# A mixed-layer kernel: most of the products into channel-by-token form, with the weights standing in the array

## The reference

```
block 1: u = rmsnorm(x) * norm_w;  proj = mm(u, w_in)
  split -> ml_q, ml_k, ml_v, ml_o, ml_z, gates, dn_q, dn_k, dn_v, dn_z, gate_a, gate_b
  mLSTM: 8 heads, q.k scores with gate decays, times v, norm, sigmoid(o)*silu(z)
  delta rule: causal conv of 4 taps over tokens on dn_q, dn_k, dn_v, then silu,
     l2norm of q and k, 16 heads in chunks, triangular solve, norm, silu(z)
  x = rmsnorm(x + sigmoid(gate_a)*mm(h_a, w_out[:2048]) + sigmoid(gate_b)*mm(h_b, w_out[2048:]))
block 2: h = rmsnorm(x)*w;  aq, ak, av, gq, gk, gv, gr, gl = split(mm(h, w_in_2))
  dilated window attention, 16 heads of 64 (aq, ak, av); gated linear attention, 4 heads (gq, gk, gv)
  x = x + mm([attention, gla], w_out_2);  h = rmsnorm(x)*w
  x = x + mm(silu(mm(h, w_gate)) * mm(h, w_up), w_down);   out = rmsnorm(x)*w
```

## Time and profile before

| what | value |
|---|---|
| time, median of 3 runs | 2382.64 us (2382.16 to 2382.72) |
| time of the profiled execution | 2382.65 us |
| its span | 2380.8 us |
| granted TensorE clock | 0.999 |
| busy PE / DVE / ACT / POOL | 2364.4 / 1425.4 / 1184.1 / 241.6 us |

### The profile page before, as it was taken

The page is one execution under the profiler, slowest core; times in us unless marked ns, Lnnn a source line. Parts: engine busy times, 40 slices in busy tenths (PEclk is TensorE's granted clock), DMA queues, the critical chain, the costliest instruction groups (busy, mean ns, idle before and its releaser), DMA issues.

```text
span 2380.8 us, 28492 instructions
## 1 busy us (share of the span) xinstructions
PE 2364.4 (99%) x11458; PEld 1938.3 (81%) x11458; DVE 1425.4 (60%) x1701; ACT 1184.1 (50%) x1695; POOL 241.6 (10%) x336
## 2 busy tenths in 40 slices
PE   9999999999999999999999999999999999999998
PEld 7888888888788888888887778788888888888886
DVE  5655665665566545665864565576554554557775
ACT  6544453454445444555645455465444444446654
POOL 0053004305300430000000010000000000000000
PEclk9999999999999999999999999999999999999999
DMA  6565457446535655666665454456555555555554
GB/s 211 194 174 164 142 177 186 155 156 182 171 127 187 177 165 168 221 207 198 209 218 191 142 179 146 155 178 226 188 187 194 189 184 193 194 181 192 193 195 141
DMA packets 240658, 430.81 MB, mean 181 GB/s; under 512 B 32180, under 2 KB 35133, under 8 KB 240526
## 3 DMA queue, kind: packets, MB, share of 16 engines
q1 hardware_dynamic: 227536, 413.38, 54.4%
q10 hardware_dynamic: 12990, 15.60, 2.1%
HBM read 423.66 MB, written 5.29 MB: 180 GB/s over the span
## 4 chain that ended last, share of the span: by engine, by line
PE 89%; POOL 5%; DVE 2%; DMA 1%; issue 1%; ACT 1%; ACTq 0%; SPq 0%; POOLq 0%; DVEq 0%
PE gemm L1311 27%; PE gemm L1313 27%; PE gemm L1312 27%; POOL arena L2264 5%; PE side L893 3%; DMA arena<-delta_blocks 1%; DVE arena L1732 1%; DVE weight_lo L1726 1%; PE side L1234 1%; PE side L981 0%; PE side L903 0%; PE side L1249 0%; PE side L1273 0%; ACT weight_hi L1339 0%; PE side L1047 0%
## 5 line engine op out<-in xcount | busy, mean ns | idle before, releaser
L1726 DVE TENSOR_TENSOR weight_lo<-weight_raw,weight_hi 128x1024 fp32r<-128x1024 f32 x780 | 969.7, 1246 | 733.5 <-ACT weight_hi L1339 732.2
L1339 ACT ACTIVATE weight_hi<-weight_raw 128x1024 fp32r<-128x1024 f32 x780 | 821.9, 1056 | 860.9 <-PE gemm L1313 820.3
L1311 PE MATMUL gemm<-weight_hi,x_hi 128*128 128x512 f32 x2368 | 942.1, 398 | 3.3 <-DVE x_lo L1732 2.1
L1313 PE MATMUL gemm<-weight_hi,x_lo 128*128 128x512 f32 x2368 | 923.1, 390 | 0.0
L1312 PE MATMUL gemm<-weight_lo,x_hi 128*128 128x512 f32 x2368 | 922.1, 389 | 0.0
L1311 PEld LDWEIGHTS gemm<-weight_hi,x_hi 128*128 128x128 f32 x2368 | 444.7, 188 | 103.4 <-issue 12.5
L1313 PEld LDWEIGHTS gemm<-weight_hi,x_lo 128*128 128x128 f32 x2368 | 444.4, 188 | 94.3
L1312 PEld LDWEIGHTS gemm<-weight_lo,x_hi 128*128 128x128 f32 x2368 | 445.1, 188 | 89.4 <-issue 1.4
L1311 PE MATMUL gemm<-weight_hi,lhs_hi 128*128 128x512 f32 x736 | 287.1, 390 | 0.0
L1313 PE MATMUL gemm<-weight_hi,lhs_lo 128*128 128x512 f32 x736 | 286.4, 389 | 0.0
L1312 PE MATMUL gemm<-weight_lo,lhs_hi 128*128 128x512 f32 x736 | 286.3, 389 | 0.0
(11 more groups left out here) (184 smaller groups left out, 1028.4 us busy)
## 6 DMA issues: line engine op xcount, KB each, us to landing
weight_raw<-in_w_in_dram SPq DMA_DIRECT2D x207, 1024.0 KB, 5.1
weight_raw<-in_w_out_dram SPq DMA_DIRECT2D x48, 1024.0 KB, 5.1
weight_raw<-in_w_gate_dram SPq DMA_DIRECT2D x44, 1024.0 KB, 5.2
weight_raw<-in_w_up_dram SPq DMA_DIRECT2D x44, 1024.0 KB, 5.2
weight_raw<-in_w_down_dram SPq DMA_DIRECT2D x44, 1024.0 KB, 5.0
arena<-rel_line ACTq DMA_DIRECT2D x8, 384.0 KB, 6.1
arena<-in_x_dram SPq DMA_DIRECT2D x4, 512.0 KB, 9.5
arena<-delta_blocks ACTq DMA_DIRECT2D x16, 128.0 KB, 5.2
```

What stands on the lines that cost most here:

```text
L1311: e.matmul(pair[i][:, :], xh[:, s], wh, start=first, stop=False)
L1313: m = e.matmul(pair[i][:, :], xl[:, s], wh, start=False, stop=last)
L1339: return e.activation(o, i, ACT.Copy, scale=scale)
L1726: return e.tensor_tensor(o, x, y, op)
```

## The change

Products of the kinds dk, dq, dv, mq, mk, gq, gk, aq, ak, fg and fu (44 jobs, list `ACROSS`) are made with 128 weight columns standing and 256 tokens moving, so that their results come with channels on the partitions. The first product of each of a job's two banks streams 256 tokens and 256 zeros (a new block `x_hi[KD]`), which opens the whole bank. The turns of these jobs (`convturn`, `chan` on PE, `fturn`) go. The norm's scale is now wanted along the free axis in every partition: `rdiag` puts the scales on the diagonal of a 128 by 128 matrix (DVE), `rrow` multiplies it by ones on PE, and DVE copies the result to `scale_rows`. DVE evicts with this row (`conv`, `chan`, `fgate`), in place of `kept` on ACT and DVE and the copies behind the turns. In the feed-forward `tanh` and `silu` read the evicted gate from SBUF, and `fact` multiplies by fu's banks and then by the row.

```diff
-    put(6, "nscale", "x")
+    put(6, "nscale", "x"), put(6, "rdiag", "x"), put(7, "rrow", "x")
     put(6, "cols")
     def kept_conv(key, slot):
-        put(slot, "kept", key)
+        put(slot, "conv", key)
         for c in (0, 2):
-            put(slot + 1, "convturn", key, c)
-            put(slot + 2 + c, "convtap", key, c)
-        put(slot + 5, "convsilu", key)
+            put(slot + 1 + c, "convtap", key, c)
+        put(slot + 4, "convsilu", key)
...
-    put(s, "nscale", "r1"), put(s, "nscale", "x2")
+    put(s, "nscale", "r1"), put(s, "nscale", "x2"), put(s, "rdiag", "x2"), put(s + 1, "rrow", "x2")
...
+            put(s + 5, "rdiag", "r2"), put(s + 6, "rrow", "r2")
     for n in range(FFN // NC):
-        put(END[f"fg{n}"], "tanh", f"fg{n}"), put(END[f"fg{n}"] + 1, "silu", f"fg{n}")
-        s = END[f"fu{n}"]
-        put(s, "fact", n), put(s + 1, "fturn", n, 0), put(s + 1, "fturn", n, 2)
+        put(END[f"fg{n}"], "fgate", n), put(END[f"fg{n}"], "tanh", f"fg{n}"), put(END[f"fg{n}"] + 2, "silu", f"fg{n}")
+        put(END[f"fu{n}"], "fact", n)
...
+        def rrow(tag):                                                       # PE
+            w.wait_ge(*at("dve:rdiag", tag))
+            p, d = open_bank("rrow", tag), blk("diag", tag)
+            for i in range(NT):
+                m = e.matmul(p[:, i * P:(i + 1) * P], ONE, d[:, i * P:(i + 1) * P], start=True, stop=True)
+            m.then_inc(sem("pe:rrow"))
...
+                if kind_of(name) in ACROSS:                                  # PE, product
+                    for q in range(NC // P):
+                        o, s = pair[q // 2][:, q % 2 * T:(q % 2 + 1) * T], slice(q * P, (q + 1) * P)
+                        if first and q % 2 == 0:
+                            e.matmul(pair[q // 2][:, :], wh[:, s], xhi[:, 0:KD + 1:KD, :], start=True, stop=False)
+                        else:
+                            e.matmul(o, wh[:, s], xh, start=False, stop=False)
+                        e.matmul(o, wh[:, s], xl, start=False, stop=False)
+                        m = e.matmul(o, wl[:, s], xh, start=False, stop=last and q % 2 == 1)
+                    continue
...
+        def conv(key):                                                       # DVE
+            x = claim("raw", key)
+            w.wait_ge(*at("dve:rrow", "x"))
+            w.wait_ge(*out_of(key))
+            for i in range(2):
+                s = tt(by_row(part(x, i)), by_row(pair_of(key)[i][:, :]), over(rrows[:, :], 1, 2), ALU.mult)
+            s.then_inc(sem("dve:conv"))
...
+        def chan(key):                                                       # DVE; aq reads the tokens backwards
+            for i in range(2):
+                    s = stt(ch[:, 2 * i:2 * i + 2, :], p, scale, over(rrows[:, :], 1, 2), ALU.mult, ALU.mult)
...
+        def fgate(n):                                                        # DVE
+            for i in range(2):
+                s = tt(by_row(part(z, i)), by_row(pair_of(f"fg{n}")[i][:, :]), over(rrows[:, :], 1, 2), ALU.mult)
...
         def fact(n):
             for i in range(NT):
-                s = stt(part(g, i), part(g, i), sq[:, i:i + 1], pair_of(f"fu{n}")[i][:, :], ALU.mult, ALU.mult)
+                s = stt(part(z, i), part(z, i), 0.5, pair_of(f"fu{n}")[i][:, :], ALU.mult, ALU.mult)
+            tt(acts_all[:, 4 * n:4 * n + 4, :], by_row(z, 4), over(rrows[:, :], 1, 4), ALU.mult).then_inc(sem("dve:fact"))
```

More of the change, by code:

```diff
@@ L207, in evictions @@
         return [("act:kept", name), ("dve:kept", name)]
+    if kind in CONVS:
+        return [("dve:conv", name)]
+    if kind in CHANS:
+        return [("dve:chan", name)]
     if kind in TANH:
         return [("act:tanh", name)]
+    if kind == "fg":
+        return [("dve:fgate", number_of(name))]
     if kind in SILU:
@@ L273, in side_table @@
         for key in (f"mq{G}", f"mk{G}"):
-            put(END[key], "kept", key)
+            put(END[key], "chan", key)
         s = END[f"dz{2 * G}"] + 18
-        for key in (f"mq{G}", f"mk{G}"):
-            for c in (0, 2):
-                put(s, "chan", key, c)
         put(s - 5, "mrhs", G)
@@ L311, in side_table @@
         put(s + 5 + n, "band", 2 * n)
-    for key in ("gq", "gk", "gv0", "gv1", "aq0", "ak0", "av0", "aq1", "ak1", "av1"):
+    for key in ("gq", "gk", "aq0", "ak0", "aq1", "ak1"):
+        put(END[key], "chan", key)
+    for key in ("gv0", "gv1", "av0", "av1"):
         put(END[key], "kept", key)
@@ L384 @@
     "attn": ("alog", "aexp", "anorm", "aturn", "apv"),
-    "ffn": ("x2load", "res2", "fact", "fturn", "res4", "fweight", "tail"),
+    "ffn": ("x2load", "res2", "fgate", "fact", "res4", "fweight", "tail"),
 }
@@ L394 @@
             "dY": ("",), "donorm": ("mean", ""), "mscore": ("w", "den"), "msq": ("mean", ""),
-            "gsum": ("end", "rest", ""), "gstate": ("first", ""), "gsq": ("mean", ""), "alog": ("b", "")},
+            "gsum": ("end", "rest", ""), "fact": ("u", ""), "gstate": ("first", ""), "gsq": ("mean", ""), "alog": ("b", "")},
     "pool": {"dinv": ("zero", "")},
@@ L398 @@
 for _engine, _names in {
[L399 to L405, removed]
+        "pe": "cols0 cols xturn rrow gate1 fsum rel1 dnorm dsc dT dX dv du0 dbu du1 do dout mdec mscore "
+              "mturn mnum mout ggate2 gsum gscore gkend gstate go gout alog aturn apv",
+        "act": "xturn sqsum kept tanh convtap convsilu dnorm dT du0 du1 donorm dout mexp mturn msq mout "
+               "ggabs ggexp ggln gkend gsq gout aexp aturn apv",
+        "dve": "cols xturn rdiag rrow kept silu gate0 gate2 fsum rel0 rel1 conv chan convtap convsilu ddecay dsc dX dv dbu do "
+               "dgate mdec mm mden mgate mgated yb yhalf ya yres x1w gload ggate0 ggate2 ggate3 gscore ggated anorm res2 res4 fgate "
+               "fweight",
         "pool": "nscale dss drhs dmask donorm dgate mrhs msq gsq anorm tail"}.items():
@@ L513, in block_table @@
             live(("ET", half, c), ("aturn", half, c), ("pe:apv", half, c))
+    for n in range(FFN // NC):
+        live(("th", f"fg{n}"), ("tanh", f"fg{n}"), ("dve:silu", f"fg{n}"))
+    for tag in ("x", "x2", "r2"):
+        live(("diag", tag), ("rdiag", tag), ("pe:rrow", tag))
     for z in range(3):
-        live(("tail", z), ("fturn", 8, 0), home=z)
+        live(("tail", z), ("fact", 8), home=z)
     return t
@@ L769, in acts_ready @@
             return [at("act:apv", k // 4, k % 4 + 1)] if k < 8 else [at("act:gout", k // 4 - 2, k % 4)]
-        return [at("act:fturn" if k % 4 == 0 else "dve:fturn", k // 4, k % 4)]
+        return [at("dve:fact", k // 4)]
     def acts_slot(idx):
@@ L781, in acts_slot @@
             return SLOT["apv", k // 4, k % 4 + 1] if k < 8 else SLOT["gout", k // 4 - 2, k % 4]
-        return SLOT["fturn", k // 4, k % 4]
+        return SLOT["fact", k // 4]
     SPLITS = {}
@@ L1084, in dout @@
             m.then_inc(sem("pe:dout"))
[L1086 to L1103, removed]
         def mdec(G, n):
@@ L1402, in tanh @@
         def tanh(key):
+            if kind_of(key) == "fg":
+                th = claim("th", key)
+                w.wait_ge(*at("dve:fgate", number_of(key)))
+                e.activation(th, blk("z", key), ACT.Tanh, scale=0.5).then_inc(sem("act:tanh"))
+                return
             hr = scale_of(NORM[JOBS[JNUM[key]][5]])[1]
@@ L1776, in nscale, with rdiag, rrow, by_row @@
                 after(tt(r, r, scale_of("r1")[0], ALU.mult))
[L1777 to L1782 removed]
+            ts(hr, r, 0.5, ALU.mult).then_inc(sem("dve:nscale"))
+        def rdiag(tag):
+            d = claim("diag", tag)
+            w.wait_ge(*at("dve:nscale", tag))
+            for i in range(NT):
+                s = ts(d[:, i * P:(i + 1) * P], IDN, scale_of(tag)[0][:, i:i + 1], ALU.mult)
+            s.then_inc(sem("dve:rdiag"))
+        def rrow(tag):
+            w.wait_ge(*at("pe:rrow", tag))
+            e.tensor_copy(rrows[:, :], bank("rrow", tag)[:, 0:T]).then_inc(sem("dve:rrow"))
+        def by_row(ap, n=2):
+            return ap.rearrange("p (c t) -> p c t", c=n)
         def kept(key):
@@ L2248, in vector_program @@
                      gscore=gscore, gstate=gstate, gsq=gsq, ggated=ggated, alog=alog, anorm=anorm, res2=res2, res4=res4,
-                     fact=fact, fturn=fturn, fweight=fweight, tail=tail)
+                     rdiag=rdiag, rrow=rrow, conv=conv, chan=chan, fgate=fgate, fact=fact, fweight=fweight, tail=tail)
         for slot in range(-AHEAD, NH + 2):
```

142 lines of the change are left out of this document (62 added, 80 removed).

## The result

The changed kernel takes 2412.63 us (median of four, 2411.51 to 2413.40) where the kernel before takes 2382.68 us in the same comparison (2382.16 to 2382.75): a ratio of 1.0126, interval 1.0114 to 1.0138. It is slower by 30 us. The forecast was 2375.4, faster by 7: the time lies inside the range, but the direction was wrong.

What follows compares the result with a forecast made beforehand. PE's gapless instruction stream was taken as the bound: -31.1 + 10.0 + 1.3 + 2.8 = -17.0 us, plus 9.7 for slow slots, from 2382.65 to 2375.4 us; range 2363 to 2415.

Steps and rivals of the forecast that it cites:

- the price of a narrow matmul with a full load: All converted jobs: 256 columns stream in 113.3 ns, a full load at 111.4 ns fits behind them.
- the slow pace: Blocks 1 and 2: 70 slots behind PE's side work run at 119.1 ns, 5.8 ns more per matmul, +9.7 us.
- the load or the hand-over of each pair binds everywhere: Rival: every narrow matmul in the kernel takes 119.1 ns, +48.5 us, 2414.1 us; chance 0.20.
- deciding point: Narrow matmuls: the gain of 17.0 us is gone at 2.0 ns more each, a pace of 115.4 ns.
- the rival at 124: Rival: load and matmul pairs are handed over at about 124 ns in all narrow matmuls, +89 us, 2455 us; chance 0.06.
- a load that holds the array for its row's length: Rival: each narrow matmul takes its load's whole 188 ns, +624 us, 2990 us; chance 0.01.
- picked up at the start: Rival: the feed-forward keeps a slow pace from its start, 24 us more, 2399.6 us; chance 0.13, shared with half-way cases.
- Turns and reversing products: PE's stream: 248 turns gone save 27.5 us and aq's reversing products 3.6 us, together -31.1 us.
- zeros: Openers of the 44 jobs: 256 zeros streamed, 2 per job, 88 x 113.3 ns, +10.0 us.
- The waits for `rdiag`: PE waits before `rrow`: 2.3 us for x2, 0.55 for x, nothing for r2; +2.8 us, bounds 2 and 5.
- DVE and ACT: DVE goes from 1425 to about 1460 us, ACT falls, and neither costs time; `weight_lo` is made 8 us before PE needs it.
- DVE too late: Rival: DVE is late for PE, +16 us on the forecast, 2391 us; chance 0.05.

Runs made afterwards that it cites:

- m1_alone: A small kernel computing nothing of the reference: PE alone in series of 96 equal matmuls; full load with 256 moving columns took 119.9 ns, with 224 columns 111.6.
- x2_narrow_old_form: The kernel before, roles and turns kept, with the 44 jobs' wide matmuls, except each job's first block, cut into 7920 of 256 columns: 2428.35 us, ratio 1.0190.
- m2_alone: PE alone again, nothing of the reference computed, with other standing and moving widths and longer series: 128 columns beside 64 standing took 60.0 ns a pair.

## Why the prediction was wrong, point by point

**The step that failed** is the price of a narrow matmul with a full load. The prediction took it as the larger of two limits, the stream's 113.3 and the load's 111.4, "so the load just fits behind the stream, by 1.9 ns", and added the slow pace in 70 side-work slots only: +9.7 us. The load's limit was right (111.6 alone with 224 columns, 111.7 in the kernel), the stream's was right with a load of 64 or 80 columns (113.4), and together they take 119.9, 6.6 ns over the larger, in every series of them and in the feed-forward with no side work near. Why the two together take more than either is not shown. The term is 8360 x 6.6 = 55 us in place of 9.7.

**The rival that had the time** was *the load or the hand-over of each pair binds everywhere*, 2414.1 us at a chance of 0.20, with the right deciding point (115.4 ns). Its pace was right within 0.8 ns; the mechanisms it named are not: the load alone is done in 111.6 ns, and pairs are handed over at 60.0. That its time fits within 2 us is in part luck: its narrow matmuls were some 7 us too cheap, and the waits and blocks 1 and 2 came out cheaper than its sum by about as much. The 60.0 ns also exclude the rival at 124, and the pace of 119.9 behind loads whose rows last 192 ns excludes a load that holds the array for its row's length. A pace *picked up at the start* of the feed-forward is out too: in `m1_alone` it is there again behind six wide matmuls. The Trainium skill, "TensorE: Matmul & The Clock Gate", section "Wait — 56ns, not 53.3ns?", led to that estimate of 124 for a pair; 60.0 ns for a load and its matmul speaks against charging both. Its estimate of 106.7 ns for a full load (section LDWEIGHTS) lies 4.9 ns under the limit measured.

**The sum again.** Turns and reversing products -31.1, zeros +9.8 (measured), `rrow` +1.3, its waits +1.1 (2.8 was said), other waits of PE -2.8 (not foreseen), narrow matmuls +55.2: +33.5, where the spans differ by 30.3. The remaining 3 us lie in blocks 1 and 2: by this sum the feed-forward costs 23.2 us, as measured, and they cost 10.3 where 7 were measured. There the wide matmuls too paid 20 to 40 ns behind side work, as the prediction noted, and that was counted twice here. `x2_narrow_old_form` points the same way (5.7 ns a matmul there, 6.6 in the feed-forward, the waits of PE included), but the cause is argued, not tried alone. The prediction's chances hold a slip beside this: its own parts give the same 0.09 and slower 0.38, not 0.10 and 0.37.

**The waits for `rdiag`** were smaller, 0.9 us for 2.3 and 0.2 for 0.55, because PE came later. Ahead of `rrow` for x2 it stood at 1239.58 us where the kernel before began slot 392 at 1233.02, 6.6 later; `nscale` ended at 1239.90 for 1234.60, only 5.3 later. The slot was right, the size was not; the prediction's last paragraph puts this wait near 1215 us, against its own. The waits that vanished (7.5 to 4.7 us) are the turns' in part, which the prediction called not on the path; in this kernel, where PE has no other gaps, each of its waits is on it.

**DVE and ACT** came out as said: 1455.7 us for "about 1460", no new wait of PE for `weight_lo` (that line is gone from the list). The rival *DVE too late* did not happen.

**What could have been seen.** The earlier trace rows had 119.1 ns steady over 22 matmuls; it was read as a disturbance from side work because the earlier trace rows were quick. For that job the trace agrees: in the changed kernel no turns stand ahead of its second half, and there it is quick, 29 distances in 3.28 us, 113.1 ns:

```profile
43.30 0.28 PE L1287 MATMUL gemm<-x_hi,weight_hi 128*48 128x256 f32 x1
...
46.58 0.28 PE L1289 MATMUL gemm<-x_lo,weight_hi 128*48 128x256 f32 x1
```

But side work is not needed for a slow pace. The same 48 standing columns took 117.2 ns with PE alone, and `m2_alone` shows that 32 have both paces with nothing beside them: a series of 96 at 113.3 ns, one of 300 at 117.8. What chooses between the two is not shown. Neither row had a full load, and the only rows that had the earlier trace rows streamed half the columns. The two limits lay within 2% of each other, and their maximum was taken for their joint price.

**Where the gain went.** A converted job of 192 narrow matmuls pays 192 x 6.6 = 1.27 us (1.09 at the 5.7 ns of blocks 1 and 2) for eight turns worth 0.89, before any zeros. So by these prices no choice of jobs gains, except the two aq jobs, whose reversing products are worth twice that: some half a us each, under what can be measured, and not tried.

## What to carry to other kernels

Halving the moving side doubles the loads; where load and stream then lie within a few per cent of each other, measure the pair, since their joint pace can be above both (119.9 from 111.6 and 113.3). On an engine without gaps a change that doubles an instruction count needs its price per instruction known to the nanosecond, from a run of exactly that shape: a PE-only series gave it here for the full load (119.9 over 96 and 120.0 over 300), but not for 32 standing columns (113.3 and 117.8), so the series should be long. Here the saving was 3.7 ns for each narrow matmul (31.1 us over 8360) and the excess 6.6.

## What the runs showed of the hardware that I had not expected

- fp32r matmuls run at 226.8 ns for 512 columns and 113.4 for 256 (the latter with 64 or 80 standing columns), bf16 at 214.0 and 108.3, at a granted clock of 0.992 to 0.996 of 2.4 GHz. The bf16 pair with a full load ran at 108.3 ns, so the limit of 111.6 belongs to the fp32r load.
- Many distances of fp32r matmuls are multiples of 6.67 ns (60.0, 66.7, 113.3, 119.9, 146.7, 173.3, 226.8), with excesses over the smooth price at widths from 264 to 480, up to 5.7 ns (288 beside 96 standing, 133.3 ns); a wide matmul behind a load of 64 columns took 230.0 ns, 3 more than behind a full one. What makes these steps stays open, and so does why, with 256 moving columns, a full load falls on 18 of them, one of 64 or 80 columns on 17, and 48, 88, 96, 104 and 112 between (117.2, 117.2, 116.1, 118.0 and 117.7 ns).
- One wide and one narrow matmul in turn, both with full loads, took 353 ns a pair where 340 is their sum at the smooth price, and 346.7 by what each takes in a series of its own: widening only every second matmul does not avoid the excess.
